# The second layer's modulation sums, the turning of x between stages, the opening and the latent norms of a two-layer fp32 transformer step, arranged anew

## The chip, the cores and the metric

The kernel runs on one core of a Trainium2 chip. The metric is the device time of one execution in microseconds. All inputs and outputs are fp32 and lie in HBM; the kernel brings in everything itself.

## What is computed

Two layers work on 128 context tokens and 256 sample tokens, D = 1024 channels. The two groups share the weights and differ in the conditioning vector and in what attention sees. Cut to what matters here:

```
mod = silu(c) @ w_mod[l] + b_mod[l]            # 6 x 1024: sh1 sc1 g1 sh2 sc2 g2, one set for context, one for samples
h = rms_norm(x, g_pre_mix) * (1 + sc1) + sh1
proj = h @ w_in                                 # latents of q and kv, rotary key, lru_x, lru_gate, merge gates
q = rms_norm(q_lat, g_q) @ w_q_up;  ckv = rms_norm(kv_lat, g_kv)
y = gates * (attention @ w_o_mla) + gates * ((rg_lru(lru_x) * gelu(lru_gate)) @ w_o_lru)
x = x + g1 * rms_norm(y @ w_out, g_post_mix)
h = rms_norm(x, g_pre_ffn) * (1 + sc2) + sh2
x = x + g2 * rms_norm((silu(h @ w1) * (h @ w2)) @ w_ffn_out, g_post_ffn)
```

## The kernel before

Every engine's program is written out by hand, with counted semaphores between them. A job is one slice of a weight matrix against all 384 tokens: `lx0`, `lx1`, `qk`, `kr`, `gg0`, `gg1`, `m2a` to `m1b` (slices of `w_in`), `qn0`, `qn1`, `kv`, `ol0` to `om1`, `wo` (the output product of the mixing block), `fi0` to `fi10` (feed-forward in) and `fo` (feed-forward out). An fp32 product is three products of fp32r numbers: high by high (L698), low activation by high weight (L705), high activation by low weight (L706), each 128x128 by 128x384. The token jobs `wo` and `fo` have tokens on the partitions and do the same three products at L801 to L803, 128x512 each, for the token tiles in the order TILES = (1, 2, 0), where tiles 1 and 2 are samples and 0 is context.

Weights come in chunks of 512 KB (two or four blocks of 128 rows) through SyncE's one queue, in the order of `plan_loads`. ScalarE makes the high half of each (`weight_high`, L1227), VectorE the low half (`weight_low`, L1607). There are three raw buffers and five split ones. Chunks of `w_mod` go through the same queue into two buffers of their own, and a chunk's transfer waits until its buffer has been used.

A modulation block is 512 of the 6144 columns of `w_mod`, r = 0 to 11. Blocks 6 to 9, the second norm's shift and scale, are the four feed-forward blocks, 4 and 5 the first gain g1, 10 and 11 the second gain g2, 0 to 3 the first norm's shift and scale. They are made in three ways. The first layer's 0 to 3 are products on TensorE in the opening (`first_product`, L881, 32 columns by 128x512, and `first_fold`, L891). Blocks 6, 7, 8, 9, 4 and 5 are products on TensorE set between the products of a job that hosts them (`MODS`; L735 in groups of sixteen, then VectorE copies them out at L1652, `mod_fold` turns them at L744, and VectorE reduces them in `mod_result`), in both layers. Blocks 10 and 11 and the next layer's 0 to 3 are summed on VectorE in the feed-forward stage, weight row block times conditioning value, added up (`sum_quarter`, L1625 and L1628, 128x512), and TensorE then only adds over the partitions: `gain_sums` at L781 and `next_sums` at L755, inside job `fo`.

Between the last product of `wo` or `fo` and the next job lies a seam: ScalarE squares y (L1235) and makes its root (L1249, L1252), VectorE multiplies y by the gain (L1744) and adds it to x (L1751), ScalarE squares x and makes rstd, and then

```
nc.scalar.activation(rstd[:, P * a:P * a + P], ident[:, :], ACT.Copy, scale=ss[:, 21 + a:22 + a])   # L1277, a diagonal
nc.tensor.matmul(turn_bank(job, c)[:, P*a:P*a+P], x[:, a, P*c:P*c+P], rstd[:, P*a:P*a+P], ...)       # L658
```

so that TensorE turns x to channels on the partitions and scales it at once, in fp32: tiles 1 and 2 for chunks c = 0 to 3 while tile 0 is still being finished (with four products into banks written again later, L850), then tile 0, then chunk 4, and 5, 6, 7 from `turn_between` inside the next job. VectorE applies scale and shift (`shifted`, L1704), ScalarE takes the high half (`act_high`, L1311), VectorE the low half (L1714). There are three seams: between mixing and feed-forward in each layer, and between the layers. In the opening the same turn is done for the first layer.

The root of the latents (`latent_norms`, L962 and L966) sums squares over the partitions, five products of a matrix of ones with 128x384 squares that ScalarE wrote, and stands inside job `m2a`. In this stage VectorE also does the recurrence (`scans`, L1857, L1861), its inputs (L1853, L1872), and the inputs of the gates.

Of the names: ybuf and ytok are one buffer seen by channels or by tokens, ss is `sums`, latent_sq is part of `sq`.

## Time and profile before

| what | before |
|---|---|
| median of 3 runs | 1290.33 us (1288.76 to 1290.85) |
| the profiled execution's own time | 1289.83 us |
| its span | 1288.0 us |
| granted clock of TensorE, mean | 0.998 |
| TensorE products busy | 1259.7 us (98%) |
| VectorE busy | 803.5 us (62%) |
| ScalarE busy | 660.5 us (51%) |
| GpSimd busy | 18.4 us (1%) |
| moved by DMA | 199.39 MB, mean 155 GB/s |

TensorE is busy nearly all the time, by a mean over stages: what an engine waits for in one stage is to be read from that stage. The span is the time from the first to the last recorded instruction, and the run's own time is 1.8 us more.

### The profile page before, as it was taken

The numbers are of one execution on the slowest core, as the hardware profiler recorded it, in microseconds if no ns is written. First come the engines' busy times: TensorE is split into PE (matmuls) and PEld (weight loads), VectorE is DVE, ScalarE is ACT, GpSimd is POOL, SyncE is SP. The second block draws the span as 40 slices with busy tenths as digits, with TensorE's granted clock in tenths as the row PEclk, the third lists the DMA queues.
The fourth block names the chain that finished last, engine by engine and source line by source line (L and its number), as shares of the span: only waits on it lengthen the run. The fifth ranks groups of instructions, "written<-read, shape, count | busy, mean of one in ns | idle before, by whom it ended". The sixth has DMA issues, their size and how long they took to land.

```text
span 1288.0 us, 20162 instructions
## 1 busy us (share of the span) xinstructions
PE 1259.7 (98%) x7748; PEld 1163.7 (90%) x7748; DVE 803.5 (62%) x1424; ACT 660.5 (51%) x1170; POOL 18.4 (1%) x41
## 2 busy tenths in 40 slices
PE   6999999999999999999999999999999999999998
PEld 4999999978889999998889999998798899999886
DVE  2697584764858877743368786756566884433423
ACT  5379873754464333342266989457445533333422
POOL 0000000200000000000000000011000000000000
PEclk9999999999999999999999999999999999999999
DMA  9645555333346766545425546463225464444451
GB/s 335 202 121 175 191 153 195 105 115 120 119 128 205 228 212 212 164 139 176 123 63 166 156 132 203 130 227 112 102 77 162 149 200 131 132 131 131 156 164 49
DMA packets 138275, 199.39 MB, mean 155 GB/s; under 512 B 10330, under 2 KB 70980, under 8 KB 138180
## 3 DMA queue, kind: packets, MB, share of 16 engines
q1 hardware_dynamic: 138180, 198.11, 48.3%
q8 instruction: 62, 1.02, 0.3%
q14 instruction: 33, 0.27, 0.1%
HBM read 196.16 MB, written 1.92 MB: 154 GB/s over the span
## 4 chain that ended last, share of the span: by engine, by line
PE 87%; DVE 5%; ACT 4%; issue 2%; DMA 2%; SPq 0%; DVEq 0%; ACTq 0%
PE bank L698 19%; PE bank L705 18%; PE bank L706 18%; PE bank L801 5%; PE bank L803 5%; PE bank L802 5%; PE bank L735 2%; DVE weight_low L1607 1%; PE bank L1096 1%; PE bank L658 1%; ACT sq L1235 1%; PE bank L1120 1%; ACT weight_high L1227 1%; PE bank L1105 1%; PE bank L939 1%
## 5 line engine op out<-in xcount | busy, mean ns | idle before, releaser
L705 PE MATMUL bank<-act_low,weight_high 128*128 128x384 f32 x1440 | 486.8, 338 | 0.6 <-DVE weight_low L1607 0.6
L706 PE MATMUL bank<-act_high,weight_low 128*128 128x384 f32 x1440 | 482.6, 335 | 0.0
L1607 DVE TENSOR_TENSOR weight_low<-raw,weight_high 128x1024 fp32r<-128x1024 f32 (+5 forms) x282 | 320.1, 1152 | 211.4 <-ACT weight_high L1227 210.7
L1227 ACT ACTIVATE weight_high<-raw 128x1024 fp32r<-128x1024 f32 (+5 forms) x282 | 272.8, 995 | 227.8 <-PE bank L803 86.6
L698 PE MATMUL bank<-act_high,weight_high 128*128 128x384 f32 x1440 | 314.6, 338 | 1.8 <-DVE t L1704 1.8
L705 PEld LDWEIGHTS bank<-act_low,weight_high 128*128 128x128 f32 x1440 | 270.9, 188 | 6.7 <-issue 4.9
L706 PEld LDWEIGHTS bank<-act_high,weight_low 128*128 128x128 f32 x1440 | 270.9, 188 | 0.0
L698 PEld LDWEIGHTS bank<-act_high,weight_high 128*128 128x128 f32 x1440 | 252.6, 188 | 8.4 <-issue 5.3
L801 PE MATMUL bank<-weight_high,hid_high 128*128 128x512 f32 x264 | 103.0, 390 | 0.0
L803 PE MATMUL bank<-weight_high,hid_low 128*128 128x512 f32 x264 | 102.8, 389 | 0.0
L802 PE MATMUL bank<-weight_low,hid_high 128*128 128x512 f32 x264 | 102.8, 389 | 0.0
L1569 ACT ACTIVATE sq<-bank 128x384 f32<-128x384 f32 x44 | 19.2, 489 | 139.8 <-PE bank L706 139.8
L2127 DVE TENSOR_TENSOR t<-bank,sq 128x384 f32<-128x384 f32 x44 | 24.5, 558 | 90.4 <-PE bank L706 87.2
L801 PEld LDWEIGHTS bank<-weight_high,hid_high 128*128 128x128 f32 x264 | 49.6, 188 | 10.6 <-issue 0.4
L803 PEld LDWEIGHTS bank<-weight_high,hid_low 128*128 128x128 f32 x264 | 49.6, 188 | 10.4
L802 PEld LDWEIGHTS bank<-weight_low,hid_high 128*128 128x128 f32 x264 | 49.6, 188 | 10.1
L1523 ACT ACTIVATE sq<-bank 128x384 f32<-128x384 f32 (+1 forms) x48 | 20.2, 420 | 55.6 <-PE bank L1105 28.4
L2068 DVE TENSOR_REDUCE negmax<-bank 128x1 f32<-128x384 f32 (+1 forms) x48 | 22.1, 464 | 31.6 <-PE bank L1096 31.4
L658 PE MATMUL bank<-rstd,x 128*128 128x128 f32 x192 | 29.7, 301 | 12.3 <-ACT rstd L1277 10.5
L658 PEld LDWEIGHTS bank<-rstd,x 128*128 128x128 f32 x192 | 26.8, 208 | 16.4 <-issue 7.8
L1628 DVE SCALAR_TENSOR_TENSOR qkv<-mod_weight,cs,qkv 128x512 f32<-128x512 f32 x56 | 38.4, 743 | 0.0
L801 PE MATMUL bank<-weight_high,act_high 128*128 128x512 f32 x96 | 37.6, 392 | 0.0
(249 smaller groups left out, 1512.7 us busy)
## 6 DMA issues: line engine op xcount, KB each, us to landing
raw<-in_w_ffn_in SPq DMA_DIRECT2D x176, 256.0 KB, 3.8
mod_weight<-in_w_mod SPq DMA_DIRECT2D x80, 512.0 KB, 4.8
raw<-in_w_in SPq DMA_DIRECT2D x72, 512.0 KB, 4.0
raw<-in_w_ffn_out SPq DMA_DIRECT2D x44, 512.0 KB, 3.8
first_mod<-in_w_mod SPq DMA_DIRECT2D x4, 2048.0 KB, 13.9
raw<-in_w_o_lru SPq DMA_DIRECT2D x16, 512.0 KB, 3.7
raw<-in_w_out SPq DMA_DIRECT2D x16, 512.0 KB, 3.7
raw<-in_w_o_mla SPq DMA_DIRECT2D x8, 512.0 KB, 4.7
```

The source lines that it names most:

```text
L658: ins = nc.tensor.matmul(turn_bank(job, c)[:, P * a:P * a + P], x[:, a, P * c:P * c + P], rstd[:, P * a:P * a + P], start=True, stop=True)
L698: nc.tensor.matmul(bank(job, g)[:, 0:T], view[0][:, kk, cols], high[:, k, :], start=k == 0, stop=False)
L705: nc.tensor.matmul(o, view[0][:, kk, cols], low[:, k, :], start=False, stop=False)
L706: ins = nc.tensor.matmul(o, view[1][:, kk, cols], high[:, k, :], start=False, stop=k == total - 1)
L735: ins = nc.tensor.matmul(bank(job, b)[32 * q:32 * q + 32, T:512], cs[:, k, :], modw[MIDX[n] % MODR][:, 512 * kk + P * b:512 * kk + P * b + P],
L801: nc.tensor.matmul(o, high[:, k, toks], view[0][:, kk, :], start=k == 0, stop=False)
L802: nc.tensor.matmul(o, high[:, k, toks], view[1][:, kk, :], start=False, stop=False)
L803: ins = nc.tensor.matmul(o, low[:, k, toks], view[0][:, kk, :], start=False, stop=k == 2 * pairs - 1)
L1227: nc.scalar.activation(high, w, ACT.Copy).then_inc(*AC.step())
L1607: nc.vector.tensor_tensor(low, w, high.bitcast(F), ALU.subtract).then_inc(*VE.step())
L1628: nc.vector.scalar_tensor_tensor(out=total(r, g), in0=w, scalar=c, in1=total(r, g), op0=ALU.mult, op1=ALU.add).then_inc(*VE.step())
L2127: nc.vector.tensor_tensor(t[c % 2][:, :], bank(f"fi{j}", 2 + g)[:, 0:T], sq[c % 4][:, :], ALU.mult).then_inc(*VE.step("hid", c))
```

## The change

Its parts, with the letters that the prediction uses:

A. In the second layer blocks 6 to 9 are no longer products hosted in `qk`, `gg1`, `m2a` and `m1a`. They are summed on VectorE in the first layer's job `fo`, two blocks at a time (1024 columns), behind the low halves of its loads 4 to 19, from sixteen chunks of 512 KB that the queue brings between the weights. TensorE adds them over the partitions (32 small products) and turns them once (`late_sums_out`, `late_rows_turned`), VectorE copies and adds the bias (`late_rows_out`, `late_mods`). The first layer's stay where they are.

B. The sums that VectorE made before are now also made in pairs of blocks, two operations of 128x1024 for each chunk in place of four of 128x512.

C. In the three seams the diagonal on ScalarE and the fp32 product are gone. VectorE scales x by rstd into ytok (`scaled`, two operations of 128x512 for each token tile), and TensorE turns that by a transpose. The opening keeps its products.

D. In the opening the second block's product and fold stand between the turns of chunks 4 to 7, and the products and folds of the other two blocks stand further apart in job `lx0`; ScalarE takes the first high half of a weight one place earlier.

E. The squares of the latents are added on VectorE first (three operations), and TensorE does two products with ones in place of five.

```diff
-SUMMED = (10, 11, 0, 1, 2, 3)
-SUM_AT = {(f"fi{1 + q * 3 // 2 // 4}", q * 3 // 2 % 4): (SUMMED[q // 4], q % 4) for q in range(24)}
+SUMMED = (10, 0, 2)
+LATE = (6, 8)
+SUM_AT = {(f"fi{1 + q * 3 // 2 // 4}", q * 3 // 2 % 4): (SUMMED[q // C], q % C) for q in range(3 * C)}
+SUM_AT.update({("fo", 4 + q): (LATE[q // C], q % C) for q in range(2 * C)})
...
+    def summed(job, i):
+        if (job, i) in SUM_AT:
+            r, k = SUM_AT[job, i]
+            loads.append(Load(("sum", r), 1, 1024, False, [("rows", "w_mod", k, 1, r * 512, 1024, 0)]))
...
+            summed("fo", 2 * i + h)
...
-        def hosts(l, r):
-
-            return r not in NEXT or l + 1 < DEPTH
+        def runs(l, kind, r):
+
+            if kind == "mod":
+                return l == 0 or r in GAINS["mix"]
+            return r in GAINS["ffn"] or l + 1 < DEPTH
...
             def turned(at, pre, job, c, tiles, *label, layer):
 
-
                 for a in tiles:
-                    pe.wait_ge(*at(AC, "diag", pre, a))
-                    ins = nc.tensor.matmul(turn_bank(job, c)[:, P * a:P * a + P], x[:, a, P * c:P * c + P], rstd[:, P * a:P * a + P],
-                                           start=True, stop=True)
+                    pe.wait_ge(*at(VE, "scaled", pre, a, c // 4))
+                    ins = nc.tensor.transpose(turn_bank(job, c)[:, P * a:P * a + P], ytok[:, a, P * c:P * c + P], ident[:, :])
...
+                    if not runs(l, "mod", r):
+                        return
...
+                def row_sums(o, pairs):
+
+                    last = 4 * len(pairs) - 1
+                    for n, r in enumerate(pairs):
+                        pe.wait_ge(*at(VE, "summed", r))
+                        for i in range(2):
+                            for g in range(2):
+                                m = 4 * n + 2 * i + g
+                                for b in range(4):
+                                    ins = nc.tensor.matmul(o[32 * b:32 * b + 32, :], one_row[:, 31 - m:63 - m],
+                                                           total(r, g)[:, 512 * i + P * b:512 * i + P * b + P], start=m == 0, stop=m == last,
+                                                           skip_group_check=True)
+                    return ins
...
+                def late_sums_out():
+
+                    row_sums(bank("fo_b", 2)[:, T:512], LATE).then_inc(*PE.step("late_sums"))
+
+                def late_rows_turned():
+
+                    pe.wait_ge(*at(VE, "late_rows"))
+                    nc.tensor.transpose(bank("fo_b", 3)[:, T:512], late_rows[:, :], ident[:, :]).then_inc(*PE.step("late_turned"))
...
-                        for c in (2, 3):
-                            nc.tensor.matmul(turn_bank(job, c)[:, P * a:P * a + P], x[:, a, P * c:P * c + P], rstd[:, P * a:P * a + P],
-                                             start=True, stop=True)
+                        for c in (2, 3, 2, 3):
+                            nc.tensor.transpose(turn_bank(job, c)[:, P * a:P * a + P], ytok[:, a, P * c:P * c + P], ident[:, :])
...
                     if i == 7:
                         first_product(1, 0)
-                        first_product(1, 1)
                     if i == 11:
                         first_fold(1, 0)
+                        first_product(1, 1)
+                    if i == 13:
                         first_fold(1, 1)
...
+                    late_turned(4)
                     first_product(0, 1)
+                    late_turned(5)
                     first_fold(0, 1)
+                    late_turned(6)
+                    late_turned(7)
...
-                    for c in range(QC):
-                        pe.wait_ge(*at(AC, "sqq", c))
-                        nc.tensor.matmul(bank("st_qkv", 0)[:, 0:T], ones[:, :], sq[c][:, :], start=c == 0, stop=c == QC - 1
-                                         ).then_inc(*PE.step("stq", c))
-                    for c in range(KC):
-                        pe.wait_ge(*at(AC, "sqq", QC + c))
-                        nc.tensor.matmul(bank("st_qkv", 1)[:, 0:T], ones[:, :], latent_sq[QC + c], start=c == 0,
-                                         stop=c == KC - 1).then_inc(*PE.step("stq", QC + c))
+                    pe.wait_ge(*at(VE, "latent_sum", "q"))
+                    nc.tensor.matmul(bank("st_qkv", 0)[:, 0:T], ones[:, :], latent_sq[0], start=True, stop=True).then_inc(*PE.step())
+                    pe.wait_ge(*at(VE, "latent_sum", "kv"))
+                    nc.tensor.matmul(bank("st_qkv", 1)[:, 0:T], ones[:, :], latent_sq[QC], start=True, stop=True
+                                     ).then_inc(*PE.step("latent_norms"))
...
-                token_job("fo", hidh, hidl, "hid_low", {2: output_sums, **({4: next_turned} if l + 1 < DEPTH else {})}, lambda: banks_free("fo_b"))
+                token_job("fo", hidh, hidl, "hid_low", {2: output_sums, **({4: next_turned, 8: late_sums_out} if l + 1 < DEPTH else {})},
+                          lambda: banks_free("fo_b"), late_rows_turned if l + 1 < DEPTH else None)
...
+                        root(7 + 2 * a, 15 + a, 21 + a, "x_root", pre, a, layer=lp)
+                        if ready is None:
+                            ac.wait_ge(*last(l, AC))
+                            nc.scalar.activation(rstd[:, P * a:P * a + P], ident[:, :], ACT.Copy, scale=ss[:, 21 + a:22 + a]
+                                                 ).then_inc(*AC.step("diag", a))
...
+                def sum_chunk(r, k):
+
+
+                    n = of_job(("sum", r))[k]
+                    if runs(l, "sum", r):
                         ve.wait_ge(*at(mod_full[MIDX[n] % MODR], "load", n))
-                        for kk in range(2):
-                            w = modw[MIDX[n] % MODR][:, 512 * kk:512 * kk + 512]
-                            for g in range(2):
-                                c = cs[:, 2 * i + kk, g:g + 1]
-                                if 2 * i + kk == 0:
-                                    nc.vector.tensor_scalar(total(r, g), w, c, None, ALU.mult).then_inc(*VE.step())
-                                else:
-                                    ve.wait_ge(VE.sem, VE.count - 1)
-                                    nc.vector.scalar_tensor_tensor(out=total(r, g), in0=w, scalar=c, in1=total(r, g),
-                                                                   op0=ALU.mult, op1=ALU.add).then_inc(*VE.step())
+                        if (r, k) == (6, 0):
+                            ve.wait_ge(*at(PE, "fi10", 3))
+                        if (r, k) == (8, 0):
+                            ve.wait_ge(*at(PE, "gain_sums", "ffn"))
+                        w = modw[MIDX[n] % MODR][:, :]
+                        for g in range(2):
+                            c = cs[:, k, g:g + 1]
+                            if k == 0:
+                                nc.vector.tensor_scalar(total(r, g), w, c, None, ALU.mult).then_inc(*VE.step())
+                            else:
+                                ve.wait_ge(VE.sem, VE.count - 1)
+                                nc.vector.scalar_tensor_tensor(out=total(r, g), in0=w, scalar=c, in1=total(r, g),
+                                                               op0=ALU.mult, op1=ALU.add).then_inc(*VE.step())
...
+                def scaled(pre, lp, a):
+
+                    ve.wait_ge(*in_layer(lp)(AC, "x_root", pre, a))
+                    own()
+                    for h in range(2):
+                        half = slice(512 * h, 512 * h + 512)
+                        nc.vector.tensor_scalar(ytok[:, a, half], x[:, a, half], ss[:, 21 + a:22 + a], None, ALU.mult
+                                                ).then_inc(*VE.step("scaled", pre, a, h, layer=lp))
...
+                    if early:
+                        scaled(pre, lp, 0)
...
                     for a in TILES:
+                        if a == 0 and pre is not None:
+                            scaled(pre, lp, 1)
                         y(a, 0)
+                        if a == 0 and pre is not None:
+                            scaled(pre, lp, 2)
                         y(a, 1)
+                        if (post, a) == ("ffn", TILES[0]) and pre is not None:
+                            late_mods()
...
+                ve.wait_ge(*at(AC, "sqq", QC + KC - 1))
+                nc.vector.tensor_tensor(latent_sq[0], latent_sq[0], latent_sq[1], ALU.add).then_inc(*VE.step())
+                nc.vector.tensor_tensor(latent_sq[QC], latent_sq[QC], latent_sq[QC + 1], ALU.add).then_inc(*VE.step("latent_sum", "kv"))
+                own()
+                nc.vector.tensor_tensor(latent_sq[0], latent_sq[0], latent_sq[2], ALU.add).then_inc(*VE.step("latent_sum", "q"))
```

The opening on TensorE, rows of before; `first_mod` is a block's weight, `rstd` the diagonal:

```order
L658 MATMUL bank<-rstd,x 128x128 x4
L913 MATMUL bank<-ident,rows_a 128x120
L914 MATMUL bank<-ident,rows_b 128x69
L891 MATMUL bank<-mod_fold,ybuf 128x2 x4
L658 MATMUL bank<-rstd,x 128x128 x12
L881 MATMUL bank<-first_mod,cs 32x512 x8
L891 MATMUL bank<-mod_fold,ybuf 128x2 x4
L698 MATMUL bank<-act_high,weight_high 128x384 x4
```

And of the change:

```order
L671 MATMUL bank<-rstd,x 128x128 x4
L951 MATMUL bank<-ident,rows_a 128x120
L952 MATMUL bank<-ident,rows_b 128x69
L928 MATMUL bank<-mod_fold,ybuf 128x2 x4
L671 MATMUL bank<-rstd,x 128x128 x3
L918 MATMUL bank<-first_mod,cs 32x512 x8
L671 MATMUL bank<-rstd,x 128x128 x3
L928 MATMUL bank<-mod_fold,ybuf 128x2 x4
L671 MATMUL bank<-rstd,x 128x128 x6
L718 MATMUL bank<-act_high,weight_high 128x384 x4
```

The product now stands behind three of the last twelve turns and its fold behind six; six turns stand between the fold and the first product of the layer.

The seam between the layers on VectorE, rows of before:

```order
L1744 TENSOR_TENSOR ybuf<-bank,gain_ffn 128x512 x2
L1751 SCALAR_TENSOR_TENSOR x<-ybuf,sums,x 128x512 x2
L1763 TENSOR_SCALAR sums<-sums 128x1
L1704 TENSOR_SCALAR t<-bank,scale,mod 128x256 x2
L1704 TENSOR_SCALAR t<-bank,scale,mod 128x128 x2
```

And of the change:

```order
L1809 TENSOR_SCALAR ybuf<-x,sums 128x512 x2
L1820 TENSOR_TENSOR ybuf<-bank,gain_ffn 128x512
L1809 TENSOR_SCALAR ybuf<-x,sums 128x512 x2
L1820 TENSOR_TENSOR ybuf<-bank,gain_ffn 128x512
L1827 SCALAR_TENSOR_TENSOR x<-ybuf,sums,x 128x512 x2
L1845 TENSOR_SCALAR sums<-sums 128x1
L1769 TENSOR_SCALAR t<-bank,scale,mod 128x256 x2
L1809 TENSOR_SCALAR ybuf<-x,sums 128x512 x2
L1769 TENSOR_SCALAR t<-bank,scale,mod 128x128 x2
```

Tiles 1 and 2 are scaled around the first half of tile 0's y, tile 0 between the shifts of the samples and its own.

The first layer's job `fo` on VectorE, rows of before:

```order
L1607 TENSOR_TENSOR weight_low<-raw,weight_high 128x1024 x9
L1688 TENSOR_TENSOR gain_row_ffn<-bank,gain_bias_ffn 128x256
L1690 TENSOR_TENSOR gain_row_ffn<-gain_row_ffn,gain_post_ffn 128x256
L1673 COPY next_mod_rows<-bank 128x128
L1607 TENSOR_TENSOR weight_low<-raw,weight_high 128x1024 x5
```

And of the change, around the same three operations:

```order
L1651 TENSOR_TENSOR weight_low<-raw,weight_high 128x1024
L1675 SCALAR_TENSOR_TENSOR late_mod_sums<-mod_weight,cs,late_mod_sums 128x1024 x2
L1753 TENSOR_TENSOR gain_row_ffn<-bank,gain_bias_ffn 128x256
L1755 TENSOR_TENSOR gain_row_ffn<-gain_row_ffn,gain_post_ffn 128x256
L1723 COPY next_mod_rows<-bank 128x128
L1651 TENSOR_TENSOR weight_low<-raw,weight_high 128x1024
L1675 SCALAR_TENSOR_TENSOR late_mod_sums<-mod_weight,cs,late_mod_sums 128x1024 x2
L1651 TENSOR_TENSOR weight_low<-raw,weight_high 128x1024
```

Behind each low half from the fifth to the twentieth now stand two operations of a sum.

## Rows read from the trace of the kernel before

**Rows 1.** The page's costliest groups: busy us, mean ns; idle us before, and releaser.

```profile
L705 PE MATMUL bank<-act_low,weight_high 128*128 128x384 f32 x1440 | 486.8, 338 | 0.6 <-DVE weight_low L1607 0.6
```

**Rows 2.** Windows: us, busy time of each engine, PE's granted clock, DMA share, GB/s.

```profile
30.00:33.00 3.00, 3.00 (x11) 3.00 (x11) 2.89 (x7) 1.16 (x3) 0.00 (x0) 0.50 1.05 386
...
378.00:565.00 187.00, 187.00 (x1084) 186.56 (x1083) 144.68 (x205) 68.72 (x96) 0.00 (x0) 1.00 0.62 195
```

**Rows 3.** The chain that ended last, opening: start us, us, what.

```profile
20.80 2.96 PE bank L658 x24
23.76 1.90 PE bank L881 x16
25.68 0.70 DVE ybuf L1771
26.52 1.04 PE bank L891 x8
...
29.35 1.25 PE bank L698 x4
30.60 0.32 PE bank L705
...
45.06 0.74 PE bank L698 x4
```

**Rows 4.** The same chain, PE's pieces in the first layer (counts include weight loads).

```profile
160.16 1.94 PE bank L962 x6
...
192.12 0.69 PE bank L698 x4
...
194.20 1.01 PE bank L735 x32
...
197.51 0.69 PE bank L698 x4
...
202.71 0.44 PE bank L744 x4
...
588.52 1.75 PE bank L755 x64
```

**Rows 5.** VectorE's timeline: start us, us, line, operation, tiles; idle before in brackets.

```profile
133.41 1.02 DVE L1872 TENSOR_TENSOR lru_i<-lru_i,xc 128x384 f32<-128x384 f32 x2
...
134.81 2.35 DVE L1607 TENSOR_TENSOR weight_low<-raw,weight_high 128x1024 fp32r<-128x1024 f32 x2
...
185.02 1.22 DVE L1607 TENSOR_TENSOR weight_low<-raw,weight_high 128x1024 fp32r<-128x1024 f32 x1
186.16 0.88 DVE L1652 COPY mod_partial<-bank 128x128 f32<-128x128 f32 x4
```

**Rows 6.** The chain again, PE's low products behind those low halves.

```profile
137.59 0.17 PE bank L705
...
186.56 0.18 PE bank L705
```

**Rows 7.** ScalarE's timeline in the same stage.

```profile
152.49 1.06 ACT L1227 ACTIVATE weight_high<-raw 128x1024 fp32r<-128x1024 f32 x1 [1.47 <-DMA raw<-in_w_in]
```

**Rows 8.** VectorE's timeline, feed-forward stage.

```profile
516.75 0.88 DVE L1625 TENSOR_SCALAR mod_partial<-mod_weight,cs 128x512 f32<-128x512 f32 x2
517.54 1.41 DVE L1628 SCALAR_TENSOR_TENSOR mod_partial<-mod_weight,cs,mod_partial 128x512 f32<-128x512 f32 x2
...
624.48 1.23 DVE L1607 TENSOR_TENSOR weight_low<-raw,weight_high 128x1024 fp32r<-128x1024 f32 x1 [2.85 <-ACT weight_high L1227]
628.56 1.23 DVE L1607 TENSOR_TENSOR weight_low<-raw,weight_high 128x1024 fp32r<-128x1024 f32 x1 [2.85 <-ACT weight_high L1227]
```

**Rows 9.** The page's DMA issues: count, KB each, median us to landing.

```profile
mod_weight<-in_w_mod SPq DMA_DIRECT2D x80, 512.0 KB, 4.8
```

**Rows 10.** The chain in the first layer's seam between mixing and feed-forward.

```profile
375.40 0.41 ACT rstd L1277
...
375.94 1.90 PE bank L658 x14
```

More of the change, by code:

```diff
@@ L97, in w @@
             loads.append(Load(job, kc, cols, True, parts))
-            if (job, i) in SUM_AT:
-                r, q = SUM_AT[job, i]
-                loads.append(Load(("sum", r), 2, 512, False, [("rows", "w_mod", 2 * q, 2, r * 512, 512, 0)]))
+            summed(job, i)
             if job in HOSTED and (i == 0 or i == 3 and job != "ol1"):
@@ L570, in _ @@
                         stores()
-                    if not load.split and not hosts(l, load.job[1]):
+                    if not load.split and not runs(l, *load.job):
                         continue
@@ L586, in _ @@
                         sp.sem_inc(sync_passed, 1)
-                    layer = l if load.split or load.job[1] not in NEXT else l + 1
+                    layer = l + 1 if load.job[0] == "sum" and load.job[1] not in GAINS["ffn"] else l
                     for part in load.parts:
@@ L740, in mod_fold @@
                 def mod_fold(r):
+                    if not runs(l, "mod", r):
+                        return
                     pe.wait_ge(*at(VE, "partial", r))
@@ L1643, in mod_partial @@
                 def mod_partial(r):
-                    if not hosts(l, r):
+                    if not runs(l, "mod", r):
                         VE.also("partial", r)
@@ L1655, in mod_result @@
                 def mod_result(r):
+                    if not runs(l, "mod", r):
+                        VE.also("mod", r)
+                        return
                     ve.wait_ge(*at(PE, "fold", r))
@@ L2144, in _ @@
                 if l + 1 < DEPTH:
+                    late_rows_out()
                     lows("lx0", 0, layer=l + 1)
```

80 lines of the change are left out of this document (43 added, 37 removed).

## The prediction, made before the changed kernel ran

> **What bounds the kernel now.** I read the page first: the low products of L705 waited 0.6 us in all for a low half of a weight [rows 1]. The windows next: from 378 to 565 PE is busy for all of 187.00 us [rows 2]. So away from the opening and the seams PE's own work is the time, and removed PE work counts as long as DVE, ACT and DMA keep up. The chain of waits shows the other kind of place: the opening, and the seam, where PE stands until rstd is ready. The timeline of DVE then shows where PE is full but DVE is too.
>
> **Opening (D).** Now block 1's product starts behind all turns: twelve turn matmuls take 2.96, the product 1.90, its fold 1.04 from 26.52, and the first layer products start at 29.35, behind t's four scalings [rows 3]. In the new order one turn set goes first (2.96 / 4 = 0.74): the product starts at 21.54 and ends at 23.44; one turn set to 24.18; the 0.70 of the copy that the fold waits for ends at about the same time; fold to 25.3. From the fold's end (27.56) to 29.35 are 1.79, so the layer products start near 27.1, 2.2 earlier, with the last two turn sets (1.48) under the 1.79. PE's clock was 0.50 from 30 to 33 [rows 2], the lower of its two levels (1.2 GHz), after PE had stood idle for most of the 1.8 us ahead of 29.35; a group of four high products cost 1.25 and a low one 0.32 [rows 3], against 0.69 [rows 4] and 0.17 [rows 6]. Eight low ones at 0.15 too much and 0.55 for the group are 1.75. With work in that gap I expect 2.4 GHz throughout. Against this, half 1's second fold moves down to position 13, so that less PE work covers the DVE and ACT work from it to 45.06, where the next chunk starts [rows 3]: I give back 0.6. Sum −2.2 −1.75 +0.6 = **−3.3**; −1.5 if the clock falls all the same.
>
> **Latent sums (E).** PE drops three of five matmuls of 128x384: 1.94 / 3 = 0.65 each [rows 4], −1.94 per layer. But DVE adds three operations of 0.51 (1.02 for two, [rows 5]) and waits for its own result once, about 1.5, in the one stretch where it has no slack: after 133.41 it goes without idle time to the low halves that end at 137.16, while PE uses the second at 137.59 [rows 5, 6]. So PE comes 0.6 or more late there, and the chain of DVE and ACT stays full to the low half that ends at 186.24, which PE needs at 186.56 or a little before. What PE saves between is then waited away. I count layer 1 at **+0.4** (bounds −1.9, all kept, and +1.0).
>
> **Layer 2 (A).** Eight groups of sixteen modulation products go. The cadence 192.12 to 194.20 is 2.08 without a group, 194.20 to 197.51 is 3.31 with it: 1.23 each [rows 4], 9.84. Sixteen fold transposes at 0.44 / 4 [rows 4] are 1.74. With the latents' 1.94, PE alone sheds 13.5. Two groups stand ahead of the full stretch: −2.46, kept. Between the gates and the end of the scans PE sheds 3 × 1.23 + 1.94 + 0.44 = 6.07, but the bound there is DVE and ACT: they lose only ACT's 1.47 wait for a transfer [rows 7] and some 0.4 of its like (those weights queue behind the modulation transfers), and some 0.5 of reductions, against the 0.6 that the latent sums add. I count −2.0 there, net. One more copy set on DVE (0.88, [rows 5]) lets the next stretch gain 0.9. After it DVE has idle time, and the last 1.23, 0.44 and 0.87 count in full: −2.5. Sum −2.46 −2.0 −0.9 −2.5 = **−8.0** (bounds −5.4, nothing of the middle, and −13.5).
>
> **First layer's output stage (A).** DVE takes 16 chunks of two operations 128x1024. Two scalings 128x512 took 0.88 and two multiply-adds 1.41 [rows 8], 0.67 each with overlap; at double width I take 1.20 each, 2.4 a chunk (bounds 2.2, and 2.9 if nothing is saved). With the low half (1.23) a slot is about 3.6, against the 4.08 between two loads, in which DVE idles for 2.85 [rows 8]. So this is hidden, if the transfers keep up: a chunk lands 4.8 after its issue [rows 9], and the queue orders weight, chunk, weight. The last chunk hangs on load 19, whose low half is made at 628.56 [rows 8], once PE has used load 14 (five split buffers); the sums would be done near 632, and PE asks for them after load 17, three loads of 4.08 on, near 639.5: seven us to spare. Over 16 slots that is 0.44 each, so a slot may grow to 4.5, and a chunk may take some 6.3 to land, before it costs anything. PE gains 32 small matmuls: 64 pieces (32 and their loads) took 1.75 [rows 4], plus a transpose at 0.13: **+2.0**, on a full PE. The pairs (B) only halve DVE's instruction count where PE is full: nothing.
>
> **Seams (C), three.** Now: ACT makes the diagonal (0.41, 375.40), PE multiplies seven tiles, 1.90 from 375.94 [rows 10], then layer products. New: DVE scales x, 0.44 for the first half (0.88 / 2, [rows 8]), in the same place, and PE transposes, 0.11 apiece: 0.8 for seven. DVE must still shift the first tile and ACT split it, so only 0.5 of the 1.1 arrives. An earlier diagonal stands in ACT's queue ahead of the squares of the last y half, whose product is already done: 0.4 less. The later turn sets of three fall from 0.74 to 0.33, three times, of which DVE, now with three more pairs of operations, passes on 0.3. **−1.2** each, −3.6 for three (bounds −2.4 and −4.2).
>
> Here a rule speaks against the change. The trace has no stretch of transposes alone; its fold transposes stand among products, at full clock. The Trainium skill, page "TensorE: Matmul & The Clock Gate", Part 4, says that transposes do not count as a busy PE in the same way and that the full clock does not engage for them. By it, the layer products behind a seam would run at the lower clock for a while, and the sum would be that of the first rival below.
>
> **Sum.** −3.3 + 0.4 − 8.0 + 2.0 − 3.6 = −12.5, against the profiled run's 1289.83: 1277.3, and I say 1277.5 (the median of the runs shown is 0.5 above that run, which I leave in the range).
>
> **Rivals.**
> 1. *The clock falls at the seams.* For about 6 us PE has only turns; before, these were multiplications, now they are transposes. If that lets the clock fall behind each seam as it fell in the opening, each costs 1.75 by the opening's rows, three 5.2: 1282.7. For: the opening's gap of 1.8 us was enough. Against: before, too, PE waited about a third of that stretch, and from 378 on, right behind such a seam, it is full at clock 1.00 [rows 2].
> 2. *All that leaves PE is gained.* DVE reorders its waits, or slack builds up: layer 2 −13.5, layer 1's latents −1.9: 1269.5. Against: the DVE timeline without idle at 133 to 137 and around 185.
> 3. *Slower: the late sums starve.* Place: first layer's output stage. Price: 16 slots; if a chunk took over 8.2 to land (slot 5.3), (5.3 − 4.08) × 16 − 7 = 12.5, the whole gain is gone, and above it the kernel is slower: at 9.2 about 1305. Only the median of 4.8 speaks to it.
> 4. *The change does nothing.* The opening and the layer 2 gain would both have to be eaten by DVE: 1289.
>
> **Chances.** Forecast 0.45, rival 1 0.35, rival 2 0.12, rival 3 0.04, rival 4 0.04. A measurement tells about 0.2%, 2.6 us. Faster 0.93, same 0.04, slower 0.03. The range 1270 to 1284 takes in rival 1 with its worse seams and rival 2 nearly; the forecast alone is 1274.5 to 1280.5.
>
> **What would show it.** (a) First layer product at 27.1, no slice of clock at 0.50 up to 35; (b) after the scans DVE's three added operations near 133 and a PE wait of 0.5 to 1 for a low half; (c) DVE slots of 3.6 at cadence 4.08 in the output stage, no PE wait there; (d) the seam from last product to first layer product 1 us shorter, clock 1.00 behind it; (e) layer 2 8 us shorter between its first product and its feed-forward part, with PE waits for DVE's low halves that did not exist before. The prediction is wrong if (e) has no such waits (rival 2) or the windows behind the seams are at 0.5 (rival 1).

## The result and the profile after

The changed kernel takes 1281.23 us (median of 4, 1280.47 to 1283.52) against 1289.55 (1288.56 to 1290.85): a ratio of 0.9938, 95% interval 0.9925 to 0.9952, 8.3 us faster. The forecast was 1277.5, range 1270 to 1284: 12.8 less than the median that was shown before it (1290.33), 12.1 less than the 1289.55 measured beside the changed kernel. The profiled execution took 1280.97 us, its span is 1278.9 us, its mean granted clock 0.997.

The page of the changed kernel, busy us and share, then the group that answers to [rows 1]:

```profile
PE 1242.3 (97%) x7457; PEld 1145.8 (90%) x7457; DVE 836.5 (65%) x1382; ACT 658.0 (51%) x1161; POOL 18.4 (1%) x41
...
L725 PE MATMUL bank<-act_low,weight_high 128*128 128x384 f32 x1440 | 487.7, 339 | 3.6 <-DVE weight_low L1651 3.6
```

PE's product time fell by 17.4 us (1259.7 to 1242.3), the span by 9.1. So almost half of what left TensorE is not in the time. Where did it go? The waits of PE, us in total, times, longest, in the changed kernel:

```profile
PE bank L679 <- DVE ybuf L1809: 6.6, 6, 1.8
...
PE bank L725 <- DVE weight_low L1651: 3.6, 5, 1.2
...
PE bank L718 <- ACT sq L1360: 2.7, 2, 2.4
...
PE bank L718 <- ACT act_high L1354: 1.2, 1, 1.2
```

3.6 us went to waits for low halves of weights (0.6 before), 2.7 to ScalarE's root of the latents (none before; 2.4 of it is one wait in layer 2, at 797), 1.2 to the first activation behind the opening's last fold. The 6.6 us are VectorE's scaling of x in the three seams, where the kernel before waited for ScalarE's diagonals. The windows show the rest, TensorE's granted clock behind the three seams (third number from the right, before DMA share and GB/s):

```profile
374.00:378.00 4.00, 3.33 (x14) 2.91 (x15) 3.53 (x8) 2.58 (x4) 0.00 (x0) 0.74 0.01 2
662.00:666.00 4.00, 3.84 (x16) 3.48 (x16) 3.53 (x8) 2.12 (x5) 0.00 (x0) 0.58 0.05 3
996.00:1000.00 4.00, 2.84 (x17) 2.43 (x18) 3.46 (x7) 3.04 (x5) 0.00 (x0) 1.00 0.00 0
```

Behind the first two seams the clock fell to its lower level (1.2 GHz) for 3.41 us each, at 375.9 and 662.7; behind the third it did not. Below, such a stretch is called a fall.

One table tells more than the sums. Both kernels make the same 5496 layer products (L718, L725, L726 and the token jobs' L837 to L839, L698 to L803 before) in the same order, so the n-th product of one can be held against the n-th of the other. Start in us, and in the last columns how much earlier (−) than in the kernel before; "filled" and the others are kernels of the experiments below. Every column is one profiled execution; the same stretch differs by up to 1 us from one to the next:

| product at | before, start | changed, start | changed | filled (e2) | without A (e7) | latents on TensorE (e4) |
|---|---|---|---|---|---|---|
| behind the opening | 44.89 | 42.81 | −2.1 | −1.9 | −1.3 | −2.2 |
| behind the scans, layer 1 | 188.49 | 187.20 | −1.3 | −0.6 | −0.4 | −2.1 |
| behind seam 1 | 390.88 | 389.65 | −1.2 | −2.1 | −1.8 | −2.9 |
| end of layer 1's output stage | 653.96 | 654.98 | +1.0 | +0.1 | −1.8 | −0.7 |
| behind seam 2 | 673.71 | 674.70 | +1.0 | −1.2 | −3.1 | −2.0 |
| ahead of seam 3 | 997.75 | 990.84 | −6.9 | −9.1 | −0.9 | −11.5 |
| behind seam 3 | 1018.27 | 1009.15 | −9.1 | −10.8 | −2.8 | −13.6 |

Term by term, differences of that column: the opening was forecast at −3.3 and measured at −2.1; the latents in layer 1 at +0.4 and +0.8; the output stage at +2.0 and +2.2; layer 2 at −8.0 and −7.9; the seams at −3.6 together, and measured at 0.0, 0.0 and −2.2.

The opening did what I described up to its end. Its chain in the changed kernel, answering to [rows 3]:

```profile
24.38 1.04 PE bank L928 x8
...
27.21 0.94 PE bank L718 x4
28.16 0.18 PE bank L725
...
40.04 0.80 PE bank L928 x8
...
42.14 0.53 ACT act_high L1354
42.81 0.93 PE bank L718 x4
```

The first layer product stands at 27.21 (forecast 27.1), and low products take 0.18 and not 0.32. But from the last fold's end (40.84) to the next chunk (42.81) TensorE has only four low products to do and then waits 1.18 us.

In layer 1 the latents' additions stand in VectorE's full stretch, answering to [rows 5], chain of the changed kernel:

```profile
131.43 0.47 DVE sq L2009
131.90 0.48 DVE sq L2010
...
132.40 0.56 DVE sq L2012
...
134.36 2.28 DVE weight_low L1651 x2
...
136.69 0.45 PE bank L981
```

They take 1.5 us, as forecast, and the chain of waits now runs through VectorE here. The output stage, VectorE's timeline, answering to [rows 8]:

```profile
603.91 2.47 DVE L1675 SCALAR_TENSOR_TENSOR qkv<-mod_weight,cs,qkv 128x1024 f32<-128x1024 f32 x2
608.48 1.23 DVE L1651 TENSOR_TENSOR weight_low<-raw,weight_high 128x1024 fp32r<-128x1024 f32 x1 [2.10 <-ACT weight_high L1269]
...
611.62 2.48 DVE L1675 SCALAR_TENSOR_TENSOR qkv<-mod_weight,cs,qkv 128x1024 f32<-128x1024 f32 x2 [1.91 <-DMA mod_weight<-in_w_mod]
```

(qkv is the name of the buffer that the sums share.) A low half takes 1.14 us from its start to that of the sums behind it, the two sums 2.47: a slot of 3.6, as forecast. One chunk came 1.91 late, and TensorE did not wait for it.

### The profile page after: what moved, and what is told of

Its sections match the earlier page's. It is cut to its first block, busy times and chain, and to the rows that moved or that the text cites. A ratio compares the mean times of both kernels' runs of the same rounds, so it can differ in the third digit from the quotient of the medians.

```text
span 1278.9 us, 19550 instructions
## 1 busy us (share of the span) xinstructions
PE 1242.3 (97%) x7457; PEld 1145.8 (90%) x7457; DVE 836.5 (65%) x1382; ACT 658.0 (51%) x1161; POOL 18.4 (1%) x41
## 4 chain that ended last, share of the span: by engine, by line
PE 78%; DVE 10%; ACT 7%; issue 2%; DMA 1%; SPq 1%; DVEq 0%; ACTq 0%
PE bank L718 16%; PE bank L725 16%; PE bank L726 16%; PE bank L837 6%; PE bank L838 6%; PE bank L839 6%; DVE weight_low L1651 3%; ACT weight_high L1269 2%; ACT sq L1277 1%; PE bank L1137 1%; DVE lru_h L1939 1%; PE bank L1161 1%; DVE lru_tau L1943 1%; PE bank L755 1%; DVE lru_i L1935 1%
## 5 line engine op out<-in xcount | busy, mean ns | idle before, releaser
L725 PE MATMUL bank<-act_low,weight_high 128*128 128x384 f32 x1440 | 487.7, 339 | 3.6 <-DVE weight_low L1651 3.6
L726 PE MATMUL bank<-act_high,weight_low 128*128 128x384 f32 x1440 | 482.6, 335 | 0.0
L718 PE MATMUL bank<-act_high,weight_high 128*128 128x384 f32 x1440 | 315.1, 339 | 4.4 <-ACT sq L1360 2.7
L725 PEld LDWEIGHTS bank<-act_low,weight_high 128*128 128x128 f32 x1440 | 271.3, 188 | 10.9 <-DVE weight_low L1651 5.8
L726 PEld LDWEIGHTS bank<-act_high,weight_low 128*128 128x128 f32 x1440 | 271.3, 188 | 0.0
L718 PEld LDWEIGHTS bank<-act_high,weight_high 128*128 128x128 f32 x1440 | 253.6, 188 | 12.0 <-issue 4.7
L837 PE MATMUL bank<-weight_high,hid_high 128*128 128x512 f32 x264 | 103.2, 391 | 0.0
L839 PE MATMUL bank<-weight_high,hid_low 128*128 128x512 f32 x264 | 102.8, 389 | 0.0
L837 PEld LDWEIGHTS bank<-weight_high,hid_high 128*128 128x128 f32 x264 | 49.6, 188 | 10.9 <-issue 0.6
L839 PEld LDWEIGHTS bank<-weight_high,hid_low 128*128 128x128 f32 x264 | 49.5, 188 | 10.3
L838 PEld LDWEIGHTS bank<-weight_low,hid_high 128*128 128x128 f32 x264 | 49.6, 188 | 10.1
L1675 DVE SCALAR_TENSOR_TENSOR qkv<-mod_weight,cs,qkv 128x1024 f32<-128x1024 f32 x42 | 52.0, 1279 | 1.9 <-DMA mod_weight<-in_w_mod 1.9
L837 PE MATMUL bank<-weight_high,act_high 128*128 128x512 f32 x96 | 37.6, 392 | 0.0
L838 PE MATMUL bank<-weight_low,act_high 128*128 128x512 f32 x96 | 37.4, 390 | 0.0
L839 PE MATMUL bank<-weight_high,act_low 128*128 128x512 f32 x96 | 37.4, 390 | 0.0
```

Source lines behind the costliest of these rows:

```text
L718: nc.tensor.matmul(bank(job, g)[:, 0:T], view[0][:, kk, cols], high[:, k, :], start=k == 0, stop=False)
L725: nc.tensor.matmul(o, view[0][:, kk, cols], low[:, k, :], start=False, stop=False)
L726: ins = nc.tensor.matmul(o, view[1][:, kk, cols], high[:, k, :], start=False, stop=k == total - 1)
L837: nc.tensor.matmul(o, high[:, k, toks], view[0][:, kk, :], start=k == 0, stop=False)
L838: nc.tensor.matmul(o, high[:, k, toks], view[1][:, kk, :], start=False, stop=False)
L839: ins = nc.tensor.matmul(o, low[:, k, toks], view[0][:, kk, :], start=False, stop=k == 2 * pairs - 1)
```

## The experiments

**e0, the changed kernel again.** No edit.

> The changed kernel once more, as the mark for the runs beside it, and to see in how many of its executions the granted clock falls behind a seam. In the profiled one it was 0.50 for 3.4 us behind the first two of three seams and 1.00 behind the third; each fall cost 1.45 us from the first product to the ninth low product. If that is the rule for this kernel (theory 1: it belongs to the change, since the kernel before shows none there), most executions have one to three falls and the median stays near 1281. Rival: the two falls were a chance of that one execution; then the mean clock of the others is that of the kernel before (0.998 and over) and the median comes out near 1278.5.

1281.20 us (1280.45 to 1282.04), ratio 0.9938 (0.9925 to 0.9950). Its profiled execution has the falls at the same two seams (377.4 and 664.1). The mean clocks of its five executions are 0.996 or 0.997. A fall of 3.4 us at half clock takes 0.0013 off the mean, and the kernel's last 1.6 to 1.9 us at half clock 0.0007. So these are about two falls in each, and one to four in the nine executions of this kernel; such a count can be off by one. The kernel before is not free of falls: its profiled execution has one at 29.8, in the opening, and the executions on this chip have means of 0.997 and 0.998, one or two falls. The profiled one shows none behind a seam. So the median speaks for theory 1; e2 and e10 settle it.

**e1, true products at the seams.**

```diff
-                    ins = nc.tensor.transpose(turn_bank(job, c)[...], ytok[:, a, P * c:P * c + P], ident[:, :])
+                    ins = nc.tensor.matmul(turn_bank(job, c)[...], ytok[:, a, P * c:P * c + P], ident[:, :], start=True, stop=True)
```

`[...]` stands for the slice of token tile a. The same is done to the eight fillers: these are turns into banks that are written again later, whose results nobody reads.

> All 32 transposes of each seam (8 fillers among them) become true fp32 products with the same identity, same data, same waits. If transposes are what lets the clock fall, it stays at 1.00 behind all seams and 1.45 us come back for each fall seen (some two of three: 2.9), against 7 turns on the path at 0.25 instead of 0.11 (about 0.5 per seam behind VectorE's work, 1.5 in all) and the later turn sets (0.3 per seam): about 1280.5, clock 0.998 or more. If it is TensorE's idle time alone (about 3 us of each seam), the falls stay and the time is about 1283.5.

1283.04 us, ratio 0.9949 (0.9937 to 0.9962). The profiled execution has a clock of 1.00 behind each seam; its one fall came at 798, behind TensorE's wait of 2.40 us for ScalarE's root of the latents (clock of the window 0.67):

```profile
374.00:378.00 4.00, 3.62 (x28) 3.43 (x28) 3.37 (x8) 3.24 (x6) 0.00 (x0) 1.00 0.01 2
...
797.00:801.00 4.00, 3.41 (x12) 3.42 (x13) 3.97 (x7) 3.94 (x8) 0.00 (x0) 0.67 0.85 249
```

All five executions have a mean of 0.998, about one fall. So with products the clock kept its level at the seams. The time is 3.9 above e2, and the starts of the products say where. Over the three seams e1 falls behind e2 by 1.9, 1.2 and 1.5 us, 4.5 in all: my price for the slower turns (1.5 and 0.9) was about half of that. The fall at 798 costs 1.6 us at once, but TensorE then does not have to wait for the low half for which it waits 0.66 in e2, and by the end of the stage only 0.3 of it is left.

Held against the kernel before, e1 gains nothing at the seams (+0.3, −0.1, −0.3), although the diagonals are gone and VectorE does the scaling; its fillers are not what delays it, for TensorE still waits 0.38 us behind them. So what part C gains is the shorter time of the transposes. Moving the scaling away from TensorE and ScalarE gives nothing that can be told by itself.

**e2, products as fillers only.**

```diff
                         for c in (2, 3, 2, 3):
-                            nc.tensor.transpose(turn_bank(job, c)[...], ytok[:, a, P * c:P * c + P], ident[:, :])
+                            nc.tensor.matmul(turn_bank(job, c)[...], ytok[:, a, P * c:P * c + P], ident[:, :], start=True, stop=True)
```

> Only the eight filler transposes of each seam, whose result is written again, become true products: eight at 0.25 for eight at 0.11, 1.1 us more in front of an idle time of 1.78 us, so no cost of its own. If the kind of work counts, or if idle time counts, the falls disappear behind some or all seams: 1278.3 with none left. If neither (falls come by chance), the time stays at 1281.2.

1279.14 us (1278.31 to 1279.39), ratio 0.9921 (0.9907 to 0.9934), 2.1 less than e0 on the same chip, no execution of one among those of the other, and the mean clock is 0.999 in four of five. The profiled execution has no fall at a seam or in a layer, only the kernel's last microseconds at the lower level. TensorE's rows of the first seam, changed kernel:

```profile
371.59 1.04 PE L888 MATMUL bank<-ident,ybuf 128*128 128x128 f32 x8
374.41 0.64 PE L679 MATMUL bank<-ident,ybuf 128*128 128x128 f32 x4 [1.78 <-DVE ybuf L1809]
...
375.86 1.56 PE L718 MATMUL bank<-act_high,weight_high 128*128 128x384 f32 x4
```

and of e2:

```profile
372.19 1.95 PE L888 MATMUL bank<-ident,ybuf 128*128 128x128 f32 x16
375.02 0.64 PE L679 MATMUL bank<-ident,ybuf 128*128 128x128 f32 x4 [0.88 <-DVE ybuf L1810]
...
376.47 0.95 PE L718 MATMUL bank<-act_high,weight_high 128*128 128x384 f32 x4
```

A true fp32 product leaves two records and a transpose one, so x16 and x8 are both eight fillers. The idle time in front of tile 0 is 0.88 and not 1.78, tile 0's turns stand 2.8 us behind the start of the fillers in both, and the first group takes 0.95 and not 1.56.

**e3, three times the transposes as fillers.**

```diff
-                        for c in (2, 3, 2, 3):
+                        for c in (2, 3) * 6:
```

> 24 filler transposes in place of eight: the idle time of 1.78 us in front of tile 0's turn is filled by work of the kind that the change uses. If idle time decides, the falls disappear as with filler products: 1278.3. If transposes do not hold the clock, they stay as often as in the changed kernel: 1281.2, or a little above if the fillers run over by a tenth or two per seam. This run against the filler products tells kind of work from amount of work.

1279.32 us (1278.14 to 1282.43), the median of e2; mean clocks 0.997, 0.998, 0.999, 0.999, 0.998: from none to two falls in an execution, where the changed kernel has one to four. The profiled one is the slowest, with two falls. One is at 43.0, behind the opening's wait of 1.18 us, far from any filler. The other began at 374.09, ahead of the added work and behind two waits, the first of them longer than in the changed kernel (1.27 us and not 0.46):

```profile
372.70 0.44 PE L679 MATMUL bank<-ident,ybuf 128*128 128x128 f32 x2 [1.27 <-DVE ybuf L1809]
373.70 0.78 PE L679 MATMUL bank<-ident,ybuf 128*128 128x128 f32 x4 [0.56 <-DVE ybuf L1820]
374.26 4.37 PE L888 MATMUL bank<-ident,ybuf 128*128 128x128 f32 x24
```

At the second seam of the same execution the 24 fillers ran at a clock of 1.00, and so did what followed:

```profile
661.50 2.78 PE L888 MATMUL bank<-ident,ybuf 128*128 128x128 f32 x24
...
665.78 0.93 PE L718 MATMUL bank<-act_high,weight_high 128*128 128x384 f32 x4
```

The third seam is like the second. So the idle time in front of tile 0 counts, and filling it with transposes brought the time back as well as eight true products did. This trace does not agree with the rule of the Trainium skill that I had weighed ("TensorE: Matmul & The Clock Gate", Part 4): at two seams TensorE had only transposes and short waits for 6.5 and 7.1 us, and the clock stayed at 1.00. Whether transposes alone would raise it again from the lower level no run shows. That products hold the clock more reliably than transposes is not shown; e2's mean clocks are a little higher (0.999 in four of five), and neither of this run's two profiled falls stands behind its fillers.

**e4, the latents back on TensorE** (on top of e2): the five products with ones, no additions on VectorE.

> With the filler products at the seams (1279.14, no falls of the clock there), the latent sums go back: five products with ones on TensorE, no additions on VectorE. By my theory the 1.94 us per layer that the sums took off TensorE are given back as waits (3.6 us of waits for low halves and 2.7 for ScalarE's root of the latents in the changed kernel, against 0.6 and none before), and in the first layer more than that (0.7): no slower than 1279.1, likely 1278.4. If the sums are worth what they took off TensorE, it is 3.9 slower: 1283.0.

1276.41 us (1275.90 to 1277.24), ratio 0.9899 (0.9885 to 0.9912), 2.7 less than e2 on the same chip, more than I expected, and again no execution of one lies among those of the other. In the table e4 is 1.5 ahead of e2 behind the scans of layer 1 (0.3 of it already behind the opening) and gains 1.6 more in layer 2; the first seam takes 0.7 back. PE's waits:

```profile
PE bank L725 <- DVE weight_low L1655: 1.3, 3, 0.6
...
PE bank L718 <- ACT sq L1364: 0.5, 1, 0.5
```

These are 1.3 and 0.5 us, where e2 has 3.6 and 3.2.

**e5, the additions on GpSimd** (on top of e2), behind ScalarE's last square.

> The three additions of the latent squares on GpSimd, which is idle there, and not on VectorE; filler products as above. If VectorE's 1.5 us in the full stretch near 133 are what costs, they come back in the first layer (0.8 behind the gates, more behind the scans) while TensorE keeps its saving: 1277.5 to 1278.4. If ScalarE and VectorE's remaining chain bound that stretch anyway, nothing: 1279.1. If GpSimd's additions slow VectorE's beside them or come late for TensorE, 1280 and more.

1279.37 us, ratio 0.9923 (0.9909 to 0.9936): no gain on e2. GpSimd's timeline, and VectorE's beside it:

```profile
107.43 1.02 POOL L657 TENSOR_TENSOR sq<-sq 128x384 f32<-128x384 f32 x1
108.53 1.22 POOL L659 TENSOR_TENSOR sq<-sq 128x384 f32<-128x384 f32 x1
```

```profile
107.80 1.07 DVE L1966 SCALAR_TENSOR_TENSOR lru_tau<-t,lru_tau 128x384 f32<-128x384 f32 x1 [2.79 <-ACT lru_r L1452]
108.79 2.04 DVE L1657 TENSOR_TENSOR weight_low<-raw,weight_high 128x1024 fp32r<-128x1024 f32 x1
```

The same two operations of VectorE take 0.56 and 1.23 in e2. So VectorE, freed of the additions, is held up 1.3 us beside the engine that does them, at the head of its full stretch; TensorE's wait for a low half near 123 is 1.16 and not 0.31. Behind the scans of layer 1 it is 0.9 ahead of the kernel before, where e2 is 0.6 and e4 2.1 ahead. A fall stands at 795.6 in this execution, behind the wait for the root of the latents, of which 0.3 us are left at the end of the stage; the mean clocks (0.996 to 0.999) are lower than e2's, so falls hide part of what this edit may give.

**e6, the opening's last fold earlier** (on top of e2).

```diff
                     if i == 11:
                         first_fold(1, 0)
-                        first_product(1, 1)
-                    if i == 13:
                         first_fold(1, 1)
```

with `first_product(1, 1)` at position 9 (that part of the diff is left out above).

> The last block's product two places earlier in the first job (position 9) and its fold at 11 beside the other, so that the products of positions 11 to 15 cover the work of VectorE and ScalarE behind the fold; filler products as above. TensorE waited 1.18 us there for act_high at 42.81: if that was the step of the opening that I had too small (0.6 given back; measured 1.8), 1.2 come back and the time is 1277.9. If VectorE's full stretch in the same layer takes it away again, 1279.1.

1277.47 us, ratio 0.9905 (0.9890 to 0.9920), 1.7 less than e2 (the two intervals overlap). The wait for act_high is gone, but the product now waits for its weights:

```profile
36.07 1.92 PE L919 MATMUL bank<-first_mod,cs 128*32 128x512 f32 x16 [0.53 <-DMA first_mod<-in_w_mod]
38.72 1.84 PE L929 MATMUL bank<-mod_fold,ybuf 128*128 128x2 f32 x16
```

By the products' starts e6 is 0.4 ahead of e2 behind the opening and 1.0 behind the scans of layer 1, and at the end, with a fall at 795.3, 0.5. Kernels with the same opening differ by up to 1.0 there (e7 and e3), so how much of the 1.7 is this edit is not shown.

**e7, part A undone** (on top of e2): layer 2's four blocks hosted on TensorE again, no sums in the output stage.

> Part A undone alone: the second layer's four blocks are products on TensorE again, and the first layer's output stage has no sums; filler products as above. My terms for A are 8.0 less, of which the latents' share was nearly all waited away, and 2.0 more: the time is 6 above, 1285.1. If everything that leaves TensorE is gained (9.84 + 1.74 - 2.0), it is 9.6 above: 1288.7. If the output stage with its transfers costs more than its 2.0, the difference is smaller than 5.5.

1287.84 us (11 executions, 1286.77 to 1288.83), ratio 0.9986 (0.9977 to 0.9994): A is worth 8.7 us (8.4 by the ratios), not 6. The table says where: between seam 1 and the end of the output stage e2 loses 2.2 and e7 nothing, and from seam 2 to seam 3 e2 gains 7.9 while e7 loses 2.2. So A gains 10.1 of the 11.6 us (9.84 and 1.74) that it takes off TensorE, and without A the latents' part costs 2.2 there.

**e8, the additions earlier on VectorE** (on top of e2), between the halves of the second `squared_roots`.

> Filler products at the seams as before. The three additions of the latent squares stay on VectorE, but stand where it waits 2.79 us for ScalarE (between the two halves of the second squared root, near 106), ahead of the stretch that it fills without a gap. If their place is what cost 2.7 us against the latents on TensorE, they now cost VectorE 0.3 at most, and the time is that of the latents on TensorE or up to 1 below, as far as TensorE does not wait its 1.94 per layer away: 1275.4 to 1276.7. If it is the sums themselves (TensorE arriving 1.94 early only to wait), 1276.4 exactly as with them on TensorE; if neither place nor sums matter, 1279.1.

1277.66 us on another chip, ratio 0.9909 (0.9896 to 0.9923), against 0.9921 of e2 and 0.9899 of e4: between the two, and not clear of either by the intervals. The profiled execution is its fastest; its span, 1274.3, is that of e4 (1274.7). VectorE has the additions for nothing: the row behind them starts at 107.55, where the same row of e2 starts at 107.70. TensorE gains 1.9 us on e4 at the latents, in each layer, and is level with it again within some twenty us; in layer 2 it waits:

```profile
792.13 0.97 PE L718 MATMUL bank<-act_high,weight_high 128*128 128x384 f32 x4 [2.40 <-ACT sq L1361]
```

A fall of the clock stands at 793 in this execution, and the mean clocks of all four are 0.997 and 0.998, those of e4 0.999 and 1.000. So the traces say that the place was the cost: behind the scans of layer 1 e8 is 2.1 ahead of the kernel before, as e4 is. The saving itself buys a wait, behind which the clock can fall.

**e9, e4 and e6 together.**

> Filler products, latents on TensorE and the earlier last fold of the opening together. They act in different stretches, so their differences should add: 1279.14 less 2.7 less 1.7 is 1274.7. If the opening's gain was only room in front of VectorE's full stretch, which the latents' removal gives as well, 1276.4.

1276.75 us, ratio 0.9900 (0.9885 to 0.9915): that of e4. The differences do not add. In the profiled execution the opening's last product waited 0.92 for its weights (0.53 in e6), and behind the opening e9 is 0.1 ahead of e4.

**e10, part C undone** in the changed kernel: diagonal and fp32 products at the seams.

> Part C alone undone in the changed kernel: diagonal on ScalarE and fp32 products with it on TensorE at the three seams, four filler products. By the trace part C gave 1.3 at the first seam, 2.1 at the third and some 1.3 at the second where the clock did not fall, 4.5 in all, and lost 1.45 for each of some two falls: undone, the clock stays at 1.00 behind the seams and the time is 1281.2 plus 1.6, 1282.8; against the kernel with filler products 3.7 more. If C was worth nothing, 1279 to 1281.

1283.49 us, ratio 0.9956 (0.9944 to 0.9969). The windows behind the seams have 1.00, and the one fall of the profiled execution stands at 799; the mean clocks are 0.998 to 1.000. Against 0.9938 of the changed kernel part C is worth 2.3 us; with filler products (0.9921) 4.5. The ratio is that of e1 (0.9949), where only the transposes are undone.

**e11, part B undone** on e4: four operations of 128x512 for each chunk.

> The kernel with filler products and the latents on TensorE, with part B undone alone: each chunk's sum is made by four operations of 128x512 and not by two of 128x1024, the same data and transfers. The changed kernel shows 2.47 us for two wide operations, the kernel before 1.41 for two narrow ones and 0.67 for each that follows, 2.75 for four: 0.3 per chunk, on VectorE, in stretches where TensorE is full and VectorE has gaps. My term for B was nothing: the ratio to the kernel before stays at 0.990. If VectorE's time counts there, 24 chunks of the feed-forward stage and 16 of the output stage cost up to 0.3 each and the ratio goes to 0.999.

1276.94 us, ratio 0.9904 (0.9888 to 0.9921), against 0.9899: B gives nothing that can be told, as forecast.

## Why the prediction was right, and where it was not

**The whole.** The kernel is faster and inside the range, and the gain is 8.3 us and not 12.8. The first rival came true in part on top of the forecast: the clock fell behind two of three seams in both profiled executions of this kernel, and the mean clocks fit about two falls in most of the others. I had said three at 1.75; it is about two at 1.2 to 1.6. I had named a clock of 0.5 behind the seams as a sign that the forecast is wrong, and by that sign it was wrong there. e2, which removes the falls, comes to 1279.1. The total came out well partly by luck: two errors in layer 2 cancel (below).

**Seams.** Right in direction, too small in size. Without falls the three give 1.6, 1.3 and 1.8 in e2, 4.7 in all against my 3.6 with bounds to 4.2; e10 and e2 say 4.5. Over the eight fall-free traces the first gives 0.3 to 1.6, the second 1.3, the third 1.8 to 2.3; the first goes with TensorE's first wait in it for VectorE's scaled x, 0.33 in e2 and 1.31 in e9. Of my three terms (faster turns 0.5, no diagonal in ScalarE's queue 0.4, later turns 0.3) e1 leaves only the turns: with true products it gains nothing on the kernel before, so the turns were sized too low and the 0.4 of the diagonal is not seen. In the changed kernel the falls took back 2.

**Opening.** The step "half 1's second fold moves down to position 13, so that less PE work covers the DVE and ACT work from it to 45.06" was mis-sized: I gave back 0.6 for it, and it is 1.8, of which the wait for act_high is 1.2. e6 shows the alternative bounded too, by the landing of the last first_mod: the wait for it is 0.53.

**Layer 2.** −8.0 was forecast and −7.9 measured, but that is luck. I had capped the gain of the middle at what VectorE and ScalarE lose. e7 shows that A gains 10.1 of 11.6, so these engines had more room than I read from rows without idle time; and e4 and e7 show that the latents' part costs 1.6 to 2.2 in that layer, where I had counted 0.6 at the gates. The two errors cancelled. The waits for low halves that I had named as a sign are there (1.24 at 764, 0.65 at 811), but the longest is one that I had not named, 2.40 for ScalarE's root of the latents. The second rival (all is gained) is near the truth for A alone, and far from it for the latents. My four parts also add up to −7.9 and not −8.0, and to −5.9 without the middle, where I had written −5.4.

**Latents, layer 1.** +0.4 was forecast, and it is +0.8 in the changed kernel and 0.7 to 1.3 in the other traces that have the additions in that place (0.0 to 0.2 with the latents on TensorE). The mechanism (VectorE late by the additions, the 1.94 waited away) is what the chain shows; the wait for a low half that I had put at 0.5 to 1 is 1.11, at 185. e8 shows both halves: moved out of the full stretch the additions cost nothing there, and then the 1.94 is waited away all the same. e5 shows only that GpSimd is no way out.

**Output stage.** +2.0 was forecast, 2.2 measured. The third rival had no ground: chunks landed in a median of 4.3 us in this stage (its 1305 for a landing of 9.2 does not follow from its own figures either: they give a slot of 5.7 and some 1297):

```profile
mod_weight<-in_w_mod SPq DMA_DIRECT2D x14, 512.0 KB, 4.3
```

**What stays open.** Whether the kind of work matters for a fall beside the idle time: e1 and e2 had none at the seams, e3 one of three, behind waits and ahead of its fillers. Why the clock falls in one execution and not in the next of the same kernel is open too, and why single executions differ by 1 us with equal clocks; the traces place such differences in the opening and the first seam, without a cause.

## What to carry to other kernels

Work that leaves the bounding engine is worth its time only where the engines that feed it have room in that stretch. Put the replacement where its engine waits anyway, and look at what comes next in the bounding engine's program: a product removed in front of a wait only makes the wait longer. Where TensorE's work at a seam becomes shorter, look at the granted clock behind it; a few true products into banks that are written again kept it up here, at no cost. Before a forecast is called right by its total, count its terms against the trace, one by one. The best version here is e4, ratio 0.9899 (0.9885 to 0.9912), with e9 and e11 level: the change without the latents' additions and with true products as fillers.

## What was not expected of the hardware

GpSimd's additions hold VectorE up: beside additions of 1.0 to 1.2 us on GpSimd, VectorE's 128x1024 low half took 2.04 us (1.23 alone), and a 128x384 operation 1.07 (0.56).

The same kernel has between one and four falls of the clock of 3.4 us each from one execution to the next, at places where TensorE has waited: behind the seams, at 43.0 in e3, and in e1, e5, e6, e8 and e10 behind the wait for ScalarE's root of the latents, near 793 to 799. That wait is 1.9 to 2.4 us in the ten traces with part E, and five of them have the fall; it is 0.45 in e4, e9 and e11, which have none there. And a fall need not cost what it takes from TensorE: the five near 795 cost 1.6 us at once and 0.3 to 0.5 at the end of the stage, where TensorE then waits less for the other engines, while the falls behind the seams of the changed kernel, with full work after them, cost 1.2 to 1.6.
